# A projection with its convolutions spread over steps, 64-byte weight rooms, and a convolution's first tap on ScalarE

## The reference

```python
u = rms_norm(hid, norm_pre_w)
proj = jnp.einsum('bsd,de->bse', u, w_in.astype(u.dtype))       # 1024 -> 6672 columns
q, k, v, g_attn, z, xbc, dt_raw = jnp.split(proj, np.cumsum(sizes).tolist(), axis=-1)
attn = mixture_of_dilations(q, k, v)                            # 16 heads
attn = attn * jax.nn.silu(g_attn.astype(jnp.float32))
xbc = jax.nn.silu(causal_depthwise_conv(xbc, conv_w, conv_b))   # 4 taps and a bias per channel
xs, b_mat, c_mat = jnp.split(xbc, [D_SSM, D_SSM + SSM_GROUPS * D_STATE], axis=-1)
dt = jax.nn.softplus(dt_raw.astype(jnp.float32) + dt_bias.astype(jnp.float32))
# ssd_chunked(...), gate with silu(z), grouped norm, output projection, norm, residual
```

## Time and profile before

| | us |
|---|---|
| median of 3 runs | 2313.26 |
| lowest and highest | 2310.68, 2316.27 |
| profiled execution, its own time | 2307.99 |
| its span, first to last instruction | 2306.2 |
| PE busy | 2177.1 (94%) |
| DVE, ACT, POOL busy | 1413.7, 997.9, 1443.9 |
| mean granted TensorE clock | 0.977 of full |

### The profile page before, as it was taken

How to read it: one execution, slowest core, us unless ns; L and a number is a source line. 1 busy time by engine, 2 the same in 40 slices (tenths; PEclk the granted TensorE clock), 3 DMA queues, 4 the chain that set the end, 5 groups by cost and what they waited for, 6 DMA issues and landing times. The chain is left out here.

```text
span 2306.2 us, 34733 instructions
## 1 busy us (share of the span) xinstructions
PE 2177.1 (94%) x12061; PEld 1835.2 (80%) x12061; DVE 1413.7 (61%) x2605; ACT 997.9 (43%) x2341; POOL 1443.9 (63%) x877
## 2 busy tenths in 40 slices
PE   5999999989999999998989999999996699999998
PEld 3778877777888888877858999999996588888876
DVE  6462236995522223499657777777777866666661
ACT  5332343333422234333336777777774423323231
POOL 6577677888667767788815556556542455555552
PEclk8999999999999999999989999999998799999999
DMA  4463332333733233322455555565547343444431
GB/s 129 151 230 105 92 106 61 108 92 128 237 107 108 97 92 110 92 73 83 137 126 114 144 126 133 139 158 137 139 115 260 103 130 128 138 129 131 140 100 55
DMA packets 260220, 287.19 MB, mean 125 GB/s; under 512 B 78420, under 2 KB 228112, under 8 KB 251984
## 3 DMA queue, kind: packets, MB, share of 16 engines
q1 hardware_dynamic: 258944, 277.50, 41.2%
q0 software_dynamic: 1104, 7.47, 0.8%
HBM read 195.28 MB, written 81.00 MB: 120 GB/s over the span
## 5 line engine op out<-in xcount | busy, mean ns | idle before, releaser
L935 PE MATMUL mm<-b_hi,w_hi 128*128 128x512 f32 x1456 | 576.3, 396 | 7.0 <-DVE fm L757 4.9
L937 PE MATMUL mm<-b_hi,w_lo 128*128 128x512 f32 x1456 | 573.0, 394 | 0.0
L936 PE MATMUL mm<-b_lo,w_hi 128*128 128x512 f32 x1456 | 572.5, 393 | 0.0
L493 POOL TENSOR_TENSOR w_lo<-w_raw,w_hi 128x512 fp32r<-128x512 f32 x208 | 315.3, 1521 | 132.1 <-ACT w_hi L567 123.9
L935 PEld LDWEIGHTS mm<-b_hi,w_hi 128*128 128x128 f32 x1456 | 274.0, 188 | 70.2 <-issue 9.4
L937 PEld LDWEIGHTS mm<-b_hi,w_lo 128*128 128x128 f32 x1456 | 273.9, 188 | 62.8
L936 PEld LDWEIGHTS mm<-b_lo,w_hi 128*128 128x128 f32 x1456 | 274.1, 188 | 61.3
L1729 PE MATMUL ps_t<-ident_b,probs 128*128 128x128 f32 x1136 | 214.6, 279 | 13.9 <-ACT probs L1660 6.8
L567 ACT ACTIVATE w_hi<-w_raw 128x512 fp32r<-128x512 f32 x208 | 129.2, 627 | 214.0 <-PE mm L937 209.2
L2214 PE MATMUL ps_out<-wo_hi,mix_hi 128*128 128x512 f32 x512 | 208.7, 408 | 1.3 <-ACT mix_hi L2165 1.3
L757 DVE SCALAR_TENSOR_TENSOR fm<-mm,u 128x512 f32<-128x512 f32 x120 | 92.0, 769 | 184.8 <-PE mm L937 184.6
(11 more groups left out here) (236 smaller groups left out, 4443.4 us busy)
## 6 DMA issues: line engine op xcount, KB each, us to landing
w_raw<-in_w_in_dram SPq DMA_DIRECT2D x52, 1024.0 KB, 5.7
feat<-fm SPq DMA_DIRECT2D x56, 512.0 KB, 5.5
tok<-tok_tile SPq DMA_DIRECT2D x52, 512.0 KB, 4.1
raw_q<-feat SPq DMA_DIRECT2D x32, 512.0 KB, 6.3
raw_k<-feat SPq DMA_DIRECT2D x32, 512.0 KB, 6.5
cum_b<-cum_scratch SPq DMA_DIRECT2D x16, 1024.0 KB, 7.8
cls_nat<-cls_out SPq DMA_DIRECT2D x64, 132.0 KB, 2.7
tok_tile<-in_x_dram SPq DMA_DIRECT2D x16, 512.0 KB, 3.8
```

Source lines behind the costliest of these rows:

```text
L493: pool.tensor_tensor(wl[o][:, :, :], source(o, n), wh[o][:, :, :].bitcast(F32), ALU.subtract)\
L935: pe.matmul(bank, w_hi[:, k, :], bh[o][:, k, :], start=(opens and k == 0), stop=False)
L936: pe.matmul(bank, w_hi[:, k, :], bl[o][:, k, :], start=False, stop=False)
L937: last = pe.matmul(bank, w_lo[:, k, :], bh[o][:, k, :], start=False, stop=(closes and k == KH - 1))
```

## The change

It does five things.

1. **Rooms.** `w_hi4`, `w_lo4`, `w_hi5`, `w_lo5` move to the front of the area behind the `b` tiles, and `TANH_AT` loses its 32 bytes. All seven pairs of weight rooms then start at multiples of 64 bytes. What lies behind `TANH_AT` (set 0 of `fm`, `w_raw1`, the two sum tiles, `ident_b`, the masks, 7 of the 16 `wo_lo`) moves by 32 bytes.
2. **Spread convolutions.** The order of the steps alternates x, b and c with q, k or v. Tile 0 of a convolved step s is convolved in step s + 1, tile 1 in step s + 2, and their transposes stand in steps s + 2 and s + 3 after product 0, 8 each. The 16 transposes of v and z stand after product 3 of the next step. The semaphores `turned` and `tok_made` are split by tile; `SETS` says which of two `fm` sets a step uses.
3. **First tap.** ACT makes it, as Identity with a scale and a bias from SBUF; three taps stay with DVE.
4. **Start and preparation.** Four rooms for token tiles instead of two, the two new ones in `raw[1]`, whose weights are loaded later; `PREP` runs in steps 0 to 3.
5. **attend.** The work on dt moves from ahead of the first masks into the first units of head 0.

```diff
-TANH_AT = CONV_AT + 8 * KB + 32
+TANH_AT = CONV_AT + 8 * KB
-ORDERS = ("qqqqkkvvvvzzzzxxxxbcggggkk", "qqqqkkkkvvvvzzzzxxxxbcgggg")
+ORDERS = ("qqqqxvxkxvxkbvckvzzzzggggk", "qxqxqxqxkbkckkvvvvzzzzgggg")
+SETS = ("00000101010101011010101010", "01010101010100010101010101")
-        self.set = 0 if n < 6 else n % 2
+        self.set = int(SETS[half][n % len(SETS[0])])
+        self.turn_at = [(n + 2 + b, 0) for b in range(2)] if self.conv else [(n + 1, 3)] * 2
+        SLOT_AT = sb.at
+        sb.at += 8 * KB
-        for rooms, group in ((sb, (4, 5)), (Rooms(nc, W_LO1_AT, FM1_AT), (6,)), ...
+        for rooms, group in ((Rooms(nc, SLOT_AT, SLOT_AT + 8 * KB), (4, 5)), (Rooms(nc, W_LO1_AT, FM1_AT), (6,)), ...
+        x_wide = raw[1][:, :, :].rearrange("p k f -> p (k f)")
+        x_rooms = [*x_tok, x_wide[:, 0:D_MODEL], x_wide[:, D_MODEL:2 * D_MODEL]]
-        RELOAD = {(TURN - 1, 1): 0, (TURN - 1, 2): 1, (TURN - 1, 3): 2, (TURN - 1, 5): 3, (TURN, 0): 4, (TURN, 1): 5,
+        RELOAD = {(TURN - 1, 1): 0, (TURN - 1, 3): 1, (TURN - 1, 4): 2, (TURN - 1, 6): 3, (TURN, 0): 4, (TURN, 1): 5,
-        PREP = {j + 1: j for j in range(LANES)}
+        PREP = {j: j for j in range(LANES)}
+        def conv_behind(n):
+            if n and steps[n - 1].conv:
+                return steps[n - 1], 0
+            if n > 1 and steps[n - 2].conv:
+                return steps[n - 2], 1
 ... SP, start
-                load_x(1)
+                for i in range(1, 3):
+                    load_x(i)
                 load_w(0)
+                load_x(3)
                 sp.dma_start(dt_raw[:, :, :], w_cols[:, :, FT * P:D_PROJ]).then_inc(dt_in, 16)
-                for i in range(2, 6):
-                    sp.wait_ge(normed, i - 1)
+                for i in range(4, HT):
+                    sp.wait_ge(normed, i - 3)
                     load_x(i)
-                load_w(1)
...
+                sp.wait_ge(u_turned, START)
+                load_w(1)
 ... ACT
+                def first_tap(s, b):
+                    at = s.tile0 + b
+                    act.wait_ge(dve_read, READS * (s.n + 1))
+                    if s.half == 1:
+                        act.wait_ge(carried, 2 * s.convs + 2)
+                    else:
+                        act.wait_ge(padded, 2)
+                    act.wait_ge(conv_step, 8 * s.convs + 4 * b)
+                    free_fm(act, s, b)
+                    act.activation(fm[s.set][b][:, :], conv_in[b][:, 0:HALF], ACT.Identity, scale=taps[:, at:at + 1],
+                                   bias=taps[:, at + CONV_K * n_conv:at + CONV_K * n_conv + 1]).then_inc(conv_step, 1)
 ... ACT, each step
+                    conv = conv_behind(n)
+                    if conv:
+                        first_tap(*conv)
                     if n:
                         read_first(s)
...
                     high(2, n + 1)
                     reload(n, 2)
+                    if conv:
+                        conv_tanhs(*conv)
                     high(3, n + 1)
+                    for part in due(n, 3):
+                        collect(*part)
 ... DVE, each step
                     if conv:
-                        bring(conv)
-                        for j in range(CONV_K):
-                            tap_step(conv, 0, j)
+                        if conv[1] == 0:
+                            bring(conv[0])
+                        for j in range(1, CONV_K):
+                            tap_step(*conv, j)
...
-                    if conv:
-                        tap_step(conv, 1, 0)
-                        tap_step(conv, 1, 1)
...
                     if conv:
-                        finish(conv, 0)
-                        tap_step(conv, 1, 2)
-                        tap_step(conv, 1, 3)
+                        finish(*conv)
...
-                    if conv:
-                        finish(conv, 1)
 ... attend, DVE
-                        if s == 4:
+                        if s == 1:
+                            take_size()
+                        if s == 5:
+                            take_one_plus()
                             take_ratio()
-                        if s == 8:
+                        if s == 10:
                             take_softplus()
-                        if s == 12:
+                        if s == 13:
                             cumulate()
 ... attend, ACT
+                    if is_first(pair) and p == 2:
+                        dt_exps()
+                    if is_first(pair) and p == 7:
+                        dt_log()
```

More of the change, by code:

```diff
@@ L159, in all_steps @@
             out.append(Step(len(out), half, kind, FIRST_PAIR[kind] + order[:i].count(kind), out[:]))
+    for s in out:
+        s.turn = [sum(t.turns and t.turn_at[b] < s.turn_at[b] for t in out) for b in range(2)]
     return out
@@ L243, in project @@
         prep_out = sem("prep_out")
-        stage_in = [sem(f"stage_in{i}") for i in range(len(stage))]
+        rows_in = [sem(f"rows_in{i}") for i in range(len(stage))]
+        X_LOADS = [6, 6, 2, 2]
         u_turned = sem("u_turned")
@@ L313, in bank, with due, free_fm @@
             return mm[(PRODUCTS * s.n + o) % BANKS]
-        def free_fm(eng, s):
+        def due(n, o):
+            return [(s, b) for s in steps if s.turns for b in range(2) if s.turn_at[b] == (n, o)]
+        def conv_behind(n):
[3 more added lines that the diff above has]
+                return steps[n - 2], 1
+            return None
+        def free_fm(eng, s, b):
             m = s.before
@@ L422, in _ @@
                             store_fm(last, b)
-                    if last2 is not None and last2.conv and last2.turns:
-                        store_tok(last2)
-                    if last is not None and last.kind in "vz":
-                        store_tok(last)
+                    for part in due(n, 0):
+                        store_tok(*part)
                     if n in PREP:
@@ L653, in _ @@
                     square(i + 2)
-                    if i < 2:
-                        high(i, 0)
-                for o in (2, 3, 4):
-                    high(o, 0)
+                    high(i, 0)
+                square(6)
+                square(7)
+                high(4, 0)
                 for j in range(LANES):
@@ L671, in _ @@
                     n = s.n
-                    last, last2 = (steps[n - 1] if n else None), (steps[n - 2] if n > 1 else None)
                     if n in PREP:
@@ L697, in _ @@
                     high(4, n + 1)
-                    if last is not None and last.conv:
-                        conv_tanhs(last, 1)
+                    reload(n, 4)
                     high(5, n + 1)
-                    reload(n, 5)
                     high(6, n + 1)
+                    reload(n, 6)
                     if s.gz:
@@ L859, in _ @@
                     last = steps[n - 1] if n else None
-                    conv = last if last is not None and last.conv else None
+                    conv = conv_behind(n)
                     if n in PREP:
@@ L1053, in _ @@
                             multiply(s, o)
-                        if o == 0 and last2 is not None and last2.conv and last2.turns:
-                            turn_tiles(last2)
-                        if o == 0 and last is not None and last.kind == "v":
-                            turn_tiles(last)
-                        if o == 1 and last is not None and last.kind == "z":
-                            turn_tiles(last)
+                        for part in due(n, o):
+                            turn_tile(*part)
                         reload(n, o)
```

196 lines of the change are left out of this document (96 added, 100 removed).

## The result

| | before | after |
|---|---|---|
| median, us | 2314.56 (4 runs) | 2248.72 (4 runs) |
| lowest and highest | 2310.68, 2316.27 | 2247.01, 2252.12 |
| profiled execution | 2307.99 | 2247.01 |
| its span | 2306.2 | 2245.3 |

The ratio is 0.972, with a 95% interval of 0.970 to 0.974: 66 us less by the medians, 60.9 by the two profiled spans. In three later sets of runs the kernel before had medians of 2309.9 to 2310.9 (7 to 9 runs each), so the gain is nearer 62 than 66. Forecast were 2259 and a gain of 54.

What follows compares the result with a forecast made beforehand. PE was taken to bound the first part, except where DVE's convolutions delay it. Gains 14.6 + 34.9 + 1.3 + 4.4 - 1.5, called 54 us, gave a 2259 us median; own range 2252 to 2266, over all 2247 to 2277.

Steps and rivals of the forecast that it cites:

- more than forecast: Rival: start gains 8, attend gains 1, aligned transposes and `ident_b` some 3 us; 2249 us in all; chance 0.10.
- What bounds the kernel: PE bounds the first part, except where DVE has 20 us of convolution in a step of 19.4.
- Rooms: Weights starting 32 bytes past a multiple of 64 slow four products by 0.07 us each; 14.6 us gained over 52 steps.
- Spread convolutions: Steps 16 to 21 and 44 to 49: all 34.9 us of PE's waits and lower clock go.
- the second rival: Convolutions still hold PE back, as DVE's chain begins waiting for ACT: 24 us at 1 us a tile step, 2283; chance 0.12.
- Start: Before step 1: four token rooms help, dt's weights come about 3.3 us later; gain 4.4 us, from 0 to 8.
- Preparation: Second half's tokens: the circle of sums, store, load, square, normalise only begins a step earlier; 0, from -3 to +3 us.
- Steps 25 and 26: Reloading under `RELOAD` keeps its 7 blocks; 0 us.
- `attend`: Earlier masks give nothing, as v bounds the first `ps_o`; table loads among running units cost 1.5 us, from -1 to +4.
- the signs that I gave for being right: Among them: plain step at 19.1 us, finish waits at most 0.5 us, DVE 70% or less, full clock until `attend`.

Runs made afterwards that it cites:

- the third edit: Changed kernel with weight slots 4 and 5 moved by 64 bytes, so their four rooms start at 64 past a multiple of 128: 2257.2 us median.

## Why the prediction was right, step by step

The time, 2248.7, lies in the range over all (2247 to 2277) and outside the forecast's own (2252 to 2266); by its number it is the rival "more than forecast", 2249.

**What bounds the kernel** held: the ledger's two large terms are those that were read from the plain steps and the waits.

**Rooms**: right in kind, 14.6 forecast and 16.8 found. Two things were mis-sized. I took product 2 with its 2.73 us for unburdened, but it stands behind products 0 and 1 and carries 0.01 of their tail; the true value is 2.72. So the four lose 0.08 each and product 2 another 0.01, which makes 0.33 a step and not 0.28. And the rule I gave for it, 64 bytes, is contradicted: by the third edit it takes at least 128. The Trainium skill's pitch from the number of columns alone ("TensorE: Matmul & The Clock Gate", section "Back-to-back issue gap") gives for 512 columns an estimate of 215.8 ns; the Trainium skill calls this the gap of an isolated matmul and gives about 131 ns for a stream of loads and matmuls of 512 columns. The rows show 227 aligned and 233 misaligned, and the measurement decides. The Trainium skill's "SBUF — State Buffer", section "Operand start alignment", knows a start only as a matter of what is legal.

**Spread convolutions**: 34.9 forecast, 34.9 found, and the price came from differences between starts of steps, where the wait rows alone would have said 25.5. DVE's share was forecast at 14.7 us a step and is 65.36 in 5.0 steps, 13.1; POOL's at 17 and is 88.44 / 5.0 = 17.7. The groups of tap 0 and of the other taps, 67 to 1119 us:

```profile
L836 DVE SCALAR_TENSOR_TENSOR fm<-conv_in,taps,fm 128x1024 f32<-128x1024 f32 x72 | 143.9, 1998 | 21.1 <-ACT fm L644 19.4
...
L644 ACT ACTIVATE fm<-conv_in,taps 128x1024 f32<-128x1024 f32 x24 | 29.7, 1237 | 10.0 <-DVE conv_in L822 9.3
```

DVE does wait for ACT at the head of its chain, 19.4 us in all, as the second rival had it, and none of it reaches PE. The ScalarE tap takes 1.24 us, where I had 1.1. By the Trainium skill ("ScalarE: Activation LUTs", "What ACT_TABLE_LOAD costs") two pointer operands add an estimate of 2 x 93 = 186 ns; tanh without them takes 1051 here, and 1237 - 1051 = 186. What I hadn't asked is whether the tap was needed: it wasn't.

**Start**: 4.4 forecast, 4.3 found, by the path described; that it fits to 0.1 is luck, as the changed start spreads over 3.8 us. ACT takes dt's weights at 14.32 instead of 11.29 (3.0 later, forecast 3.3), and DVE's last five splits end at 56.6 (forecast 56.5):

```profile
53.50 3.08 DVE L764 TENSOR_TENSOR b_lo<-turn,b_hi 128x512 fp32r<-128x512 f32 x5 [0.95 <-ACT b_hi L614]
```

**Preparation**: 0 forecast with 3 either way; it cost 2.3. Starting the circle a step earlier gives it no slack.

**Steps 25 and 26**: I gave `RELOAD` nothing and it cost 1.6. Product 6 of step 26 comes 1.5 us late. Exchanging the sets didn't change it. The trace names another cause. The change also moved DVE's split of the last reloaded block, `reload(n, 2)`, from ahead of the read of S3 to behind the fifth read. So this split (`b_lo`) ends at 616.47 us, and PE's first load of product 6, which needs it, stands at 616.54:

```profile
614.00 2.47 DVE L764 TENSOR_TENSOR b_lo<-turn,b_hi 128x512 fp32r<-128x512 f32 x4
...
616.54 0.19 PEld L968 LDWEIGHTS mm<-b_hi,w_hi 128*128 128x128 f32 x1 [1.59 <-issue]
```

In the kernel before the split began 13.5 us into the step, here 20.6. I overlooked this move, and no run put it back.

**`attend`**: the step that failed, by its sign. I had costed the table load that moves among running units and left out what else stands in those units. PE does wait for them, 1.0 and 1.1 us at the two table loads, but it no longer waits 5.1 us for DVE behind `cumulate`. How much that is worth isn't sharp: head 0 took 53.1 to 57.4 us in five profiles with the old placement and 49.1 to 51.8 in eight with the new one. v was the bound of the first `ps_o`, as forecast:

```profile
PE ps_o L1785 <- DMA v_nat<-tok: 9.0, 1, 9.0
```

so the earlier masks gave nothing there.

**The output part**: not in my sum at all. The ledger of moved tiles named 7 `wo_lo` rooms, and I had asked about starts only for weights. That was worth 3.4 us. The rival "more than forecast" gave 2249 for a start of 8, attend at +1 and 3 us for aligned transposes. That this number came out is luck, as its reasons didn't: start 4.3, attend 3.5, transposes -0.7, output 3.4.

Of the signs that I gave for being right, most came: the first `ps_o` stands 14.2 us behind the last product of dt, and DVE is busy 49 to 67% in each stretch of 30 to 40 us from 120 to 350 us. The clock was not full throughout: it was granted at half, 1.2 GHz, from 121.0 to 124.4 us, behind PE's waits in the preparation.

Of the 10 us between 2259 and 2248.7, 7 are the terms above, and most of the rest is the 5.3 us that I added for the distance from a profiled execution to its median, which after the change is 1.7.

## What to carry to other kernels

When identical instructions differ by 3% from one buffer to the next, compare the buffers' addresses before anything else, and try several powers of two before naming the rule. Before two remedies for one wait are built, ask what each leaves for the other: here the order alone removed all of it, and faster products gave nothing where another engine was the bound. And list every tile that a change of addresses moves, with each operand that is read from it, since the smallest of those moves paid 3.4 us.

## What the runs showed of the hardware

- A matmul 128x512 in fp32r, with its weight load, comes every 226.7 ns in the changed kernel, where the weights start at multiples of 512 bytes and the moving operands at multiples of 1 KB, and every 233.3 ns when the weights start at 32, 64 or 96 past a multiple of 128. A moving operand at 32 past costs as well (451.4 against 448.0 us for 15 chunks). Starts at 128 or 256 bytes past a multiple of 512 were not tried.
- The price isn't per load. One misaligned load in three costs 68 of 80 ns per product, and after the last one the pitch stays irregular (225 to 236 ns) for seven to ten matmuls, 30 to 53 ns in all. The same tail (46 ns in step 17) follows a hold-up with all operands aligned. In the kernel before the tail was shorter behind product 1 (11 ns) and absent behind product 5; what decides that stays open.
- A DVE TENSOR_SCALAR and a TENSOR_TENSOR_SCAN on SBUF stood still while POOL's instruction ran, ending 0.15 to 0.16 and 0.55 us after it, in the runs shown; the scan took 3.71 and 3.80 us beside POOL and 0.69 without it.
- DVE's taps with two SBUF inputs go by POOL too. In the kernel before all 72 of them end 1.08 to 1.09 us after a POOL instruction ends, in the kernel after 67 of 72, with durations from 1.29 to 2.40 us. The number of tiles in a step isn't what decides: the mean was 2218 ns before and 1998 after, but 2195 with one tile a step and the first tap on DVE, and 2076 with two and the tap on ScalarE. No run took POOL's work away.
